# Attention in a hybrid block on one core: the second key group of tiles 7 to 15 multiplies unsplit float32 probabilities

## What is computed

```
q: 8 heads x 64, k, v the same; c = cumsum(log_sigmoid(f_logit + b_forget))
for each block of 128 queries [q0, q1), with all keys [0, q1):
    logits = q k^T * 64 ** -0.5 + c[q] - c[k]      (-inf where key > query)
    p = softmax(logits)
    o = p v
```

## Time and profile before

| | us |
|---|---|
| runs | 2968.98, 2958.32, 2956.97 |
| median | 2958.32 |
| the profiled execution | 2960.12 |
| its span, first to last instruction | 2958.5 |
| attend in it, start of the first turn to start of the last values | 1013.9 to 1511.0 |

### The profile page before, as it was taken

One profiled execution on the slowest core, in us unless ns is written; L12 is line 12 of the kernel. 1 busy time (PEld: TensorE's weight loads), 2 busy tenths in 40 slices (PEclk: granted clock), 3 DMA queues, 4 the chain that ended last, 5 costly groups with the idle time before them and its releaser, 6 DMA issues. The chain is left out here.

```text
span 2958.5 us, 40365 instructions
## 1 busy us (share of the span) xinstructions
PE 2551.0 (86%) x12303; PEld 2031.1 (69%) x12303; DVE 1759.7 (59%) x2512; ACT 1057.9 (36%) x1542; POOL 616.0 (21%) x534
## 2 busy tenths in 40 slices
PE   4999999999999398999957786999199999999976
PEld 3888889889987387877845565777166666666642
DVE  6585674877721487877855553344366666666641
ACT  4110101134421376767743221212144444444420
POOL 3121322221110011111101321011322233333321
PEclk9999999999999699999978988999599999999998
DMA  5121211123231533334237777746179998988973
GB/s 127 54 86 35 78 57 64 57 86 108 93 111 60 145 88 88 88 88 121 68 92 180 184 180 215 233 152 227 62 264 351 348 359 346 351 336 347 351 278 127
DMA packets 230575, 494.39 MB, mean 167 GB/s; under 512 B 34829, under 2 KB 154765, under 8 KB 193965
## 3 DMA queue, kind: packets, MB, share of 16 engines
q1 hardware_dynamic: 189986, 387.17, 40.0%
q0 software_dynamic: 32240, 58.98, 5.9%
q10 hardware_dynamic: 8226, 46.73, 3.9%
HBM read 423.79 MB, written 125.60 MB: 186 GB/s over the span
## 5 line engine op out<-in xcount | busy, mean ns | idle before, releaser
L91 PE MATMUL project_bank<-project_xnT_hi,project_w_hi 128*128 128x512 f32 (+4 forms) x1352 | 510.9, 378 | 0.9 <-DVE project_xnT_lo L593 0.7
L92 PE MATMUL project_bank<-project_xnT_lo,project_w_hi 128*128 128x512 f32 (+4 forms) x1352 | 498.9, 369 | 0.0
L93 PE MATMUL project_bank<-project_xnT_hi,project_w_lo 128*128 128x512 f32 (+4 forms) x1352 | 496.9, 368 | 0.0
L641 DVE SCALAR_TENSOR_TENSOR project_work<-project_work,project_taps 128x2048 f32<-128x2048 f32 x128 | 341.4, 2667 | 18.6 <-DVE project_work L637 0.6
L2318 DVE TENSOR_TENSOR experts_gu_lo<-weights_gate_up,experts_gu_hi 128x2048 fp32r<-128x2048 f32 x128 | 288.1, 2289 | 50.2 <-ACT experts_gu_hi L2260 48.8
L2260 ACT ACTIVATE experts_gu_hi<-weights_gate_up 128x2048 fp32r<-128x2048 f32 x128 | 244.2, 1909 | 160.0 <-DMA weights_gate_up<-in_w_up_dram 133.9
L91 PEld LDWEIGHTS project_bank<-project_xnT_hi,project_w_hi 128*128 128x128 f32 (+1 forms) x1352 | 251.7, 186 | 35.6 <-issue 6.7
L92 PEld LDWEIGHTS project_bank<-project_xnT_lo,project_w_hi 128*128 128x128 f32 (+1 forms) x1352 | 251.7, 186 | 33.0 <-issue 6.1
L93 PEld LDWEIGHTS project_bank<-project_xnT_hi,project_w_lo 128*128 128x128 f32 (+1 forms) x1352 | 251.8, 186 | 26.8
L2222 PE MATMUL experts_y_bank<-weights_down,experts_hT 128*128 128x512 f32 x544 | 252.9, 608 | 19.5 <-issue 18.8
L1013 DVE TENSOR_TENSOR attend_pT<-attend_t_bank,attend_pT 128x512 fp32r<-128x512 f32 (+3 forms) x352 | 212.5, 615 | 86.0 <-ACT attend_pT L963 83.6
(11 more groups left out here) (259 smaller groups left out, 4398.5 us busy)
## 6 DMA issues: line engine op xcount, KB each, us to landing
weights_gate_up<-in_w_gate_dram SPq DMA_DIRECT2D x68, 1024.0 KB, 9.3
weights_gate_up<-in_w_up_dram SPq DMA_DIRECT2D x68, 1024.0 KB, 14.5
weights_down<-in_w_down_dram SPq DMA_DIRECT2D x68, 1024.0 KB, 8.3
project_w_raw<-in_w_in_dram SPq DMA_DIRECT2D x36, 512.0 KB, 3.9
qk_d<-project_work SPq DMA_DIRECT2D x16, 1032.0 KB, 5.3
gate_d<-project_work ACTq DMA_DIRECT2D x16, 1024.0 KB, 3.9
merge_gates<-gate_d SPq DMA_DIRECT2D x64, 256.0 KB, 5.2
merged_d<-merge_m_pair SPq DMA_DIRECT2D x64, 256.0 KB, 4.2
```

Of the source, the lines that this page charges most:

```text
L91: pe.matmul(out, lhs[0], rhs[0], start=first, stop=False)
L92: pe.matmul(out, lhs[0], rhs[1], start=False, stop=False)
L93: return pe.matmul(out, lhs[1], rhs[0], start=False, stop=last)
L641: nc.vector.scalar_tensor_tensor(out=work[:, 2, 0:SEQ], in0=work[:, 1, META - 1 + q:META - 1 + q + SEQ], scalar=taps[:, bass.ds(ct, 1), q] ...
```

## The change

In a tile of seven or more (three to five groups) the group g = 1 becomes "plain". ACT copies its four turned blocks as ordinary float32 into a new buffer `pT_plain`; DVE makes no low part of it; PE multiplies each block with the values read as ordinary float32, 128 columns instead of 256, into the half of the output bank that belongs to the high part. The waits follow: times_values of such a group, and the turn that takes its bank again three groups later, wait for ACT's `hi_done`; `lo_done` now counts only the groups that are not plain, by the table `LOWS`. Nine tiles of sixteen qualify, so there are 9 such groups in a head pass and 72 in all, with 288 of the 1216 values matmuls.

```diff
+        pT_plain = sb("pT_plain", [P, 3, 4, P])
...
+        def plain(u, g):
+
+            return g == 1 and TILE[u] + 2 > 8
+
+        LOWS = [sum(not plain(*GROUP[i]) for i in range(j)) for j in range(PAIR_GROUPS + 1)]
+
+        def lows(it, j):
+
+            return it * LOWS[PAIR_GROUPS] + (LOWS[max(0, j)] + 1)
...
-                pe.wait_ge(lo_done, before(it, j))
+                if j >= 3 and plain(*GROUP[j - 3]):
+                    pe.wait_ge(hi_done, it * PAIR_GROUPS + (j - 2))
+                else:
+                    pe.wait_ge(lo_done, lows(it, j - 2))
...
-                pe.wait_ge(lo_done, it * PAIR_GROUPS + (j + 2))
                 out = o_bank[:, (u // 2) % 2, (u % 2) * 2 * P:(u % 2 + 1) * 2 * P]
                 last = TILE[u] + 1
+                if plain(u, g):
+                    pe.wait_ge(hi_done, it * PAIR_GROUPS + (j + 1))
+                    for t in range(4 * g, 4 * g + 4):
+                        m = nc.tensor.matmul(out[:, 0:P], raw(values[:, h, t, :]), pT_plain[:, j % 3, t % 4, :],
+                                             start=False, stop=False)
+                    m.then_inc(pv_done, 1)
+                    return
+                pe.wait_ge(lo_done, lows(it, j + 1))
...
-                nc.scalar.activation(pT[:, j % 3, 0:n, 0, :],
+                nc.scalar.activation(pT_plain[:, j % 3, 0:n, :] if plain(u, g) else pT[:, j % 3, 0:n, 0, :],
...
+                if plain(u, g):
+                    return
                 dve.wait_ge(hi_done, it * PAIR_GROUPS + (j + 1))
```

More of the change, by code:

```diff
@@ L934, in _ @@
             pe.wait_ge(inv_done, 1)
-            pe.wait_ge(lo_done, PAIRS * PAIR_GROUPS + 1)
+            pe.wait_ge(lo_done, lows(PAIRS, 0))
             nc.tensor.transpose(t_bank[:, 0, 0:P], inv_sum[:, :], ident[:, :]).then_inc(inv_done, 1)
```

## The result

| | before | after |
|---|---|---|
| median of six runs each, us | 2962.3 (2957.0 to 2969.0) | 2974.5 (2968.4 to 2978.4) |
| ratio to before | | 1.0031, 95% interval 1.0019 to 1.0043 |
| the profiled execution, us | 2960.1 | 2976.5 |
| attend, start of the first score to start of the last values matmul, us | 508.1 | 512.9 |

The changed kernel is slower, by 9 us (6 to 13) of the 17 forecast. The two medians of this table are 12 us apart; the ratio compares runs made side by side, so I go by the ratio. Three measurements of the changed kernel give 1.0031, 1.0027 and 1.0029.

A forecast was written before the change was run, and what follows sets the result against it. No engine is full: attend is bound by a ring of PE turn, ACT copy, DVE low part and PE values. Per head pass 3 x 0 + 2 x 0.25 + 4 x 0.42 = 2.2 us, 17.4 for eight; 2958.3 + 17 = 2975, range 2960 to 2994.

The forecast's parts named there:

- DVE's relief elsewhere: Attend, tiles 10 to 7 and turns between head passes: DVE's freed time buys nothing, no gain counted.
- The price of a plain group: PE in attend: four plain matmuls become 8 records of 0.12 us, 1.04 us a group, 0.48 more than before.
- low bound: PE in attend: records at the transposes' pace, 0.11 us; a group about 0.96 us, 0.40 more, 28.8 us in all.
- Tiles 15, 14, 13 at 0: Attend's long tiles: PE's 0.75 us of idleness before the last score takes in the 0.48 us; cost 0.
- rival 1: Attend's long tiles: idle times only move, so all 34.6 us of new PE work show, 2993 us; chance 0.15.
- Tiles 12 and 11 at 0.25 each: Attend: delay passes through ACT's copies, but the wait for the own low part, 0.2 to 0.3 us, goes; 0.25 us each.
- Tiles 10, 9, 8, 7 at 0.42 each: Attend's three-group tiles: PE has no gap, so 0.48 us less a small remainder of idleness shows, 0.42 us each.
- rival 2: Attend: DVE's freed 0.6 us per group shortens take_scores to score, PE's idleness pays most; about 0, 2959 us; chance 0.14.
- PE pays everything: Attend: if idle times in long tiles only move, all 34.6 us of added PE work show, 2993 us; chance 0.15.
- It disappears: Attend: PE's 33.9 us of waits for DVE before scores and values pay most of 34.6; 2959 us; chance 0.14.
- Faster by DVE's backlog: Attend: DVE's backlog holds the ring, 52.6 us of weight loads' waits go, 18 us gained, 2940 us; chance 0.06.
- Weight loads that stand free: PE in attend: loads not hidden under matmuls, about 0.20 us a record, 1.04 more a group, 3016 us; chance 0.05.

The follow-up runs named there:

- low_kept: Changed kernel, but DVE still makes all 352 low parts and PE waits for them as before; attend 518.3 us, ratio 1.0059 to the kernel before.
- no_low_256: Changed kernel without the 72 low parts, but PE's float32r matmuls of 256 columns as before (high part twice); attend 501.7 us, ratio 0.9987 to the kernel before.
- long_only: Changed kernel with plain second groups only in tiles 11 to 15 (40 of 72); attend 508.2 us, ratio 1.0010 to the kernel before.
- high_only: Changed kernel with the 72 groups' high part alone, float32r matmuls of 128 columns, no low part; attend 501.2 us, ratio 0.9980 to the kernel before.

## Why the prediction was right and wrong

Right in its direction and inside its range, and none of the four rivals came true. But attend, which alone was reasoned about, lost 4.5 us where 17.4 were forecast. In the prediction's own terms (the 0.25 us at tiles 12 and 11 are its 0.48 less the wait for the low part, 0.23), us:

| term | forecast | measured | from |
|---|---|---|---|
| PE's work that shows, tiles 12 and 11 (16 groups) | 7.7 | 4.4 | low_kept |
| PE's work that shows, tiles 10 to 7 (32 groups) | 13.4 | 5.8 | low_kept |
| DVE's relief at tiles 12 and 11 | -3.7 | -4.3 | no_low_256 |
| DVE's relief elsewhere | 0 | -2.1 | no_low_256 |
| by which the halves fail to add | | +0.7 | after |
| sum | 17.4 | 4.5 | |

**The price of a plain group: two records for each matmul as forecast, the size too large.** Their pace was mis-sized. PE after, in a gapless stretch of three group tiles:

```profile
1075.57 0.60 PE L909 MATMUL attend_t_bank<-attend_ident,attend_probs 128*128 128x128 f32 x4
1076.00 1.06 PE L924 MATMUL attend_o_bank<-attend_pT_plain,attend_values 128*128 128x128 f32 x8
1076.81 0.48 PE L893 MATMUL attend_s_bank<-attend_keys,attend_q_hi 128*128 128x512 f32 x1
1077.13 0.39 PE L897 MATMUL attend_s_bank<-attend_keys,attend_q_lo 128*128 128x512 f32 x1
```

and a place of the same form before, with tile 10's second group for tile 8's, which continues (turn at 1116.96, values at 1117.32):

```profile
1117.88 0.39 PE L882 MATMUL attend_s_bank<-attend_keys,attend_q_hi 128*128 128x512 f32 x1
1118.11 0.39 PE L886 MATMUL attend_s_bank<-attend_keys,attend_q_lo 128*128 128x512 f32 x1
```

From the values to the next score it is 0.81 us against 0.56, only 0.25 more. But the plain values start 0.43 after the turn instead of 0.36, and the score's first matmul takes 0.32 instead of 0.23. From turn to second score it is 1.56 against 1.15, so **0.41 us** for a group, not the 0.48 of the text; its low bound was 0.40. In the same place after (tile 10 of the second head) it is 1.57. The eight records stand 0.111 us apart, the first step included, while a split set takes 0.20 for its first step and 0.118 for the others. So the record has the pace of the transposes (the low bound). 72 x 0.41 = 29.5 us of work instead of 34.6.

**Tiles 15, 14, 13 at 0: right.** The table has 0.00 to 0.01. The unit of tile 13 after, which answers the earlier trace rows:

```profile
1099.61 1.69 ACT L975 ACTIVATE attend_probs<-attend_scores,attend_low 128x1680 f32<-128x1680 f32 x1
1099.64 1.06 PE L924 MATMUL attend_o_bank<-attend_pT_plain,attend_values 128*128 128x128 f32 x8
...
1101.29 0.97 ACT L984 ACTIVATE attend_pT<-attend_t_bank 128x384 fp32r<-128x384 f32 x2
...
1101.80 0.56 DVE L1036 TENSOR_TENSOR attend_pT<-attend_t_bank,attend_pT 128x384 fp32r<-128x384 f32 x1 [1.36 <-ACT attend_pT L984]
...
1102.28 0.56 DVE L1025 CUSTOM_DVE_ANT_0 attend_scores<-attend_s_bank,attend_decay 128x400 f32<-128x400 f32 x1
...
1102.90 0.33 PE L893 MATMUL attend_s_bank<-attend_keys,attend_q_hi 128*128 128x128 f32 x1 [0.47 <-DVE attend_low L1025]
```

From ACT's exponential to the last score it is 3.29 us, as before (1094.23 to 1097.52). PE's idleness there shrank from 0.75 to 0.47, and the plain group is paid out of it. That is rival 1 refuted at its place.

**Tiles 12 and 11 at 0.25 each: the wait right, the work too large.** With DVE as before they cost 0.43 and 0.12, 0.55 together (low_kept), where the text had the full 0.48 each: part of the work is hidden there, too. DVE's relief takes back 0.54 in the first head pass and 0.57 in the second (column no_low_256), near the 0.2 to 0.3 each of the text. In the changed kernel the two together cost nothing (-0.11 and -0.03); long_only, 40 groups, has 0.1 us in all where the sum had 4.0.

**Tiles 10, 9, 8, 7 at 0.42 each: right for 10 and 7, wrong for 9 and 8.** In low_kept they cost 0.40 and, for tile 7 in the first head, 0.40; tiles 9 and 8 cost 0.19 and 0.24, and tile 9 in the second head 0.05. The step rested on one row, PE 13.00 of 13.00 us busy. That window holds one part of one head pass, tile 10 and the unit before it, and the durations of matmuls overlap their followers, so a busy PE can hide some tenths of idleness. Before, in the first head's tiles 9 and 8, where PE runs through the scores of the next head's long tiles:

```profile
1322.04 0.57 PE L909 MATMUL attend_o_bank<-attend_pT,attend_values 128*128 128x256 f32 x3
1322.95 0.33 PE L882 MATMUL attend_s_bank<-attend_keys,attend_q_hi 128*128 128x144 f32 x1 [0.35 <-DVE attend_low L1004]
```

The row says 0.35 us idle; three values matmuls need 0.20 + 2 x 0.12 = 0.44, so PE could have gone on at 1322.48 and stood free 0.47. Not all of it can be used. In the changed kernel (counted from tile 9's first turn) the turn at 1320.12 comes 0.28 us later; on it hang ACT's copy, DVE's low part and the take_scores that this score waits for, and low part and score come 0.19 later, while the idleness of 0.35 has grown to 0.53. So the group costs 0.19, about half.

**PE's part of the sum.** low_kept has 10.2 us, 1.3 a head pass, against 2.2 with the relief already taken off. For tiles 10 to 7 alone it is 5.8 against 13.4. Most of this lies in the second head, where tile 9 costs 0.05 and tiles 8 and 7, whose stretch is the turn from one round to the next, nothing that can be told from its scatter (at the very end of attend, where no next round follows, 0.7 us). The smaller price of a group is the lesser share, 0.07 x 32 = 2 us.

**DVE's relief: the wait at the values right at tiles 12 and 11, missed elsewhere.** The text had most of the 12.2 us of waits of values for DVE at first groups, which keep their low part. By the idle times that is so. The distances of starts say more: between the turn ahead and the plain group's values no_low_256 has 0.03 us, the kernel before 0.20 at tile 12, 0.49 at tile 11 (here with an idle time of only 0.22) and, where no_low_256 has 0.12, 0.50 at tile 7 of the second head. Tile 11 of the second head, before:

```profile
1108.94 0.71 PE L909 MATMUL attend_o_bank<-attend_pT,attend_values 128*128 128x256 f32 x4 [0.20 <-DVE attend_pT L1013]
1109.49 0.27 PE L895 MATMUL attend_t_bank<-attend_ident,attend_probs 128*128 128x128 f32 x1
1109.98 0.74 PE L909 MATMUL attend_o_bank<-attend_pT,attend_values 128*128 128x256 f32 x4 [0.22 <-DVE attend_pT L1013]
```

and the last two steps in no_low_256:

```profile
1111.45 0.27 PE L909 MATMUL attend_t_bank<-attend_ident,attend_probs 128*128 128x128 f32 x1
1111.48 0.72 PE L924 MATMUL attend_o_bank<-attend_pT,attend_values 128*128 128x256 f32 x4
```

and in the changed kernel:

```profile
1114.90 0.28 PE L909 MATMUL attend_t_bank<-attend_ident,attend_probs 128*128 128x128 f32 x1
1115.02 1.05 PE L924 MATMUL attend_o_bank<-attend_pT_plain,attend_values 128*128 128x128 f32 x8
```

What goes at tiles 12 and 11, 0.17 and 0.46 us a head pass, is the plain group's own wait for its low part, which the prediction named, and it is the greater part of the 6.4 us (4.3 of them). What it did not go through is the row of DVE itself: a take_scores that stands behind a low part moves up by 0.6 us, and where a score waits for it, PE moves up as well. Before, in tile 9 of the second head, where the scores of the next round begin (DVE, then PE):

```profile
1123.20 0.69 DVE L1013 TENSOR_TENSOR attend_pT<-attend_t_bank,attend_pT 128x512 fp32r<-128x512 f32 x1
...
1123.80 0.34 DVE L1004 CUSTOM_DVE_ANT_0 attend_scores<-attend_s_bank,attend_decay,attend_low 128x128 f32<-128x128 f32 x1
...
1124.21 0.45 PE L882 MATMUL attend_s_bank<-attend_keys,attend_q_hi 128*128 128x400 f32 x1 [0.73 <-DVE attend_low L1004]
```

The low part at 1123.20 is the plain group's and goes; the score at 1124.21 waits for the take_scores behind it. It can, because the first score of a round waits longer than for the group three before: `before` gives the count of all 88 groups of the last round there. no_low_256 gains 0.44 in this stretch in the first three rounds and 0.00 in the fourth, where no next round begins. This chain was rival 2's, and rival 2's argument against itself ("the low part removed stands before the burst") holds for tiles 15 to 13 and not here.

**The rivals.** PE pays everything: refuted, 10.2 of 29.5 us without DVE's part and 4.5 with it. It disappears: nearest to what attend shows, since 25 of 29.5 us are gone, yet not all; PE's waits for DVE gave 12.2 us of the 33.9 it counted on. Faster by DVE's backlog: refuted, DVE's relief alone brings 6.4 us and not 52.6. Weight loads that stand free: refuted by 0.111 us a record, against the 0.20 it needed.

That the whole program's 8 to 9 us stand nearer to the forecast is luck: 4 of them lie in merge and route, of which the prediction said that they only shift, and their cause is open.

## What to carry to other kernels

Replacing a split matmul by a plain one trades a pass of the vector engine for weight loads on TensorE: count the loads (here 288 more, 0.10 us each), since the number of columns hardly mattered at 128 and 256. Take TensorE's room from the idle time of its loads and from distances of starts, for each kind of place, never from a busy share of its matmuls in one window; an idle time of 0.22 us stood for a wait of 0.46. And when an engine that isn't the bound is relieved, look for the instruction that stands in its row behind the one removed and ask who waits for that.

## What was not expected of the hardware

- Plain float32 records of 128 columns follow each other every 0.111 us, from the first on; float32r matmuls of 256 columns every 0.118, of 128 columns every 0.111, both behind a longer first step. The Trainium skill's page "TensorE: Matmul & The Clock Gate", section "LDWEIGHTS (loading the stationary operand)", gives a load's ns as its columns divided by 1.2, an estimate of 107 ns for 128 columns. The pace of all three forms here agrees with that. For the narrow float32r form high_only speaks for the load as the bound; for the other two the runs don't tell it from the stream.
- The next instruction pays for a group, too: the score behind eight plain records took 0.09 us longer up to its second matmul, the one behind the narrow group of high_only 0.05 us.
- Project's program is the same everywhere, yet attend's first score behind it began at 1000.9 to 1002.9 us in four of the twelve profiles and at 1006.0 to 1008.0 in the other eight, and at 1002.9 and 1007.5 in two profiles of the kernel before. Attend repeated to 0.6 us. A few microseconds of a kernel like this can only be measured in the stage where they arise.
